# The order in which the last projection streams its 512 weight columns, changed in each of its four groups

## The reference

```python
def conv_ffn(h, w_up, conv_w, w_down):
    ...
    gate, val = jnp.split(c, 2, axis=-1)
    return (jax.nn.silu(gate) * val) @ w_down          # (256, 5632) @ (5632, 2048)
...
        x = x + rms_norm(conv_ffn(h, ffn_w_up[i], ffn_conv[i], ffn_w_down[i]), norm_g[i, 3])
```

## Time and profile before

| | us |
|---|---|
| median of 3 runs (2315.87, 2316.13, 2316.15) | 2316.13 |
| span of the profiled execution | 2315.1 |
| what lies around the span (median less span) | 1.0 |
| PE busy in the span | 2301.6 |
| DVE busy | 1535.4 |
| ACT busy | 1074.0 |
| first start of the last projection's matmuls | 2058.82 |
| start of its last matmul | 2307.46 |

### The profile page before, as it was taken

The page is one execution under the profiler, slowest core; times in us unless marked ns, Lnnn a source line. Parts: engine busy times, 40 slices in busy tenths (PEclk is TensorE's granted clock), DMA queues, the critical chain, the costliest instruction groups (busy, mean ns, idle before and its releaser), DMA issues.

```text
span 2315.1 us, 49304 instructions
## 1 busy us (share of the span) xinstructions
PE 2301.6 (99%) x19362; PEld 2100.1 (91%) x19362; DVE 1535.4 (66%) x1976; ACT 1074.0 (46%) x1365; POOL 111.5 (5%) x144
## 2 busy tenths in 40 slices
PE   9999999999999999999999999999999999999998
PEld 9999999999999999998889999899888888888887
DVE  5688877748766666665444867648877877774444
ACT  5543344455444444443444555655444444444343
POOL 2000000012000000000000200012000000000000
PEclk9999999999999999999999999999999999999999
DMA  7554334455666666666666574465655565666664
GB/s 253 172 165 123 119 103 125 132 196 173 192 184 183 187 186 184 181 191 187 187 189 184 156 246 128 121 198 155 191 190 191 180 196 176 192 189 201 190 184 153
DMA packets 115833, 406.94 MB, mean 176 GB/s; under 512 B 13008, under 2 KB 17968, under 8 KB 115312
## 3 DMA queue, kind: packets, MB, share of 16 engines
q1 hardware_dynamic: 110672, 396.03, 55.4%
q10 hardware_dynamic: 5024, 8.87, 1.1%
HBM read 402.70 MB, written 2.15 MB: 175 GB/s over the span
## 4 chain that ended last, share of the span: by engine, by line
PE 95%; DVE 2%; DMA 1%; POOL 1%; ACT 1%; issue 0%; DVEq 0%; POOLq 0%; ACTq 0%
PE ps L1895 25%; PE ps L1897 13%; PE ps L1900 8%; PE ps L1901 8%; PE ps L1902 8%; PE ps L2548 4%; PE ps L2549 4%; PE ps L2550 4%; PE ps L2094 3%; PE ps L2084 2%; PE ps L2085 2%; PE ps L2086 2%; PE ps L1859 2%; PE ps L1858 2%; PE ps L1857 2%; PE ps L2450 1%
## 5 line engine op out<-in xcount | busy, mean ns | idle before, releaser
L1047 DVE TENSOR_TENSOR wl<-raw,wh 128x1024 fp32r<-128x1024 f32 x742 | 906.1, 1233 | 653.2 <-ACT wh L581 651.7
L581 ACT ACTIVATE wh<-raw 128x1024 fp32r<-128x1024 f32 x742 | 776.0, 1057 | 885.1 <-PE ps L1897 362.1
L1895 PE MATMUL ps<-x,wh 128*128 128x512 f32 x1280 | 448.2, 393 | 0.8 <-DVE wl L1047 0.8
L1900 PE MATMUL ps<-xx,wh 128*128 128x258 f32 (+3 forms) x1336 | 379.9, 284 | 2.1 <-DVE xx L1080 1.2
L1901 PE MATMUL ps<-xx,wh 128*128 128x258 f32 (+3 forms) x1336 | 378.3, 283 | 0.0
L1902 PE MATMUL ps<-xx,wl 128*128 128x258 f32 (+3 forms) x1336 | 377.8, 283 | 0.0
L1897 PE MATMUL ps<-x,wl 128*128 128x256 f32 x1280 | 357.1, 279 | 0.0
L1895 PEld LDWEIGHTS ps<-x,wh 128*128 128x128 f32 x1280 | 239.8, 187 | 58.6 <-DVE wl L1047 1.1
L1900 PEld LDWEIGHTS ps<-xx,wh 128*128 128x128 f32 x1336 | 251.3, 188 | 4.7 <-DVE wl L1047 2.3
L1901 PEld LDWEIGHTS ps<-xx,wh 128*128 128x128 f32 x1336 | 251.3, 188 | 0.4
L1902 PEld LDWEIGHTS ps<-xx,wl 128*128 128x128 f32 x1336 | 251.4, 188 | 0.0
(11 more groups left out here) (354 smaller groups left out, 3848.8 us busy)
## 6 DMA issues: line engine op xcount, KB each, us to landing
raw<-in_gate_up SPq DMA_DIRECT2D x176, 512.0 KB, 3.6
raw<-in_down SPq DMA_DIRECT2D x176, 512.0 KB, 4.2
raw<-in_up SPq DMA_DIRECT2D x176, 512.0 KB, 3.9
raw<-in_w_in SPq DMA_DIRECT2D x103, 512.0 KB, 3.7
raw<-in_in SPq DMA_DIRECT2D x48, 512.0 KB, 3.6
raw<-in_w_out SPq DMA_DIRECT2D x32, 512.0 KB, 4.4
raw<-in_out SPq DMA_DIRECT2D x32, 512.0 KB, 3.7
bias<-bias_rows ACTq DMA_DIRECT2D x1, 4096.0 KB, 26.5
```

Source lines behind the costliest of these rows:

```text
L581: act.activation(wh[:, slot], raw[:, slot], ACT.Copy).then_inc(high_ready, 1)
L1047: dve.tensor_tensor(wl[:, slot], raw[:, slot], wh[:, slot].bitcast(F32), ALU.subtract).then_inc(low_ready, 1)
L1895: pe.matmul(ps[:, 4 * parity + m, :].rearrange("p (s n) -> p s n", s=2), w_high, hi, start=(k == 0), stop=False)
L1900: pe.matmul(out, w_high, high, start=(k == 0), stop=False)
```

## The change

Each group of `down2` gets an entry of the table `STREAM`: a number of streams, a run length, and a side. The 512 columns are cut into so many streams, and the walk takes a run from each in turn. For "read" the address pattern of the streaming operand does this: with two streams of 16 it reads columns 0 to 15, 256 to 271, 16 to 31, 272 to 287, and so on, and the sums go to PSUM as before, one after the other. The host stores the weight columns so that each lands in its place. For "write" the weights are read one after the other, and the address pattern of the output in PSUM jumps in the same manner. Group 0 reads two streams of 16, group 1 two of 8, group 2 writes two of 16, group 3 reads four of 32. No instruction is added, removed or moved, no wait and no semaphore changes, and the chunks have the same size and order. Every matmul of the four groups has 512 columns as before.

```diff
+STREAM = [(2, 16, "read"), (2, 8, "read"), (2, 16, "write"), (4, 32, "read")]
+
+def _streamed(chunks):
+    chunks = chunks.reshape(4, -1, P, 2, 512)
+    out = np.empty_like(chunks)
+    for g, (parts, run, _) in enumerate(STREAM):
+        order = np.arange(512).reshape(parts, -1, run).transpose(1, 0, 2).reshape(-1)
+        if STREAM[g][2] == "read":
+            out[g][..., order] = chunks[g]
+        else:
+            out[g] = chunks[g][..., order]
+    return np.ascontiguousarray(out.reshape(-1, P, 2, 512))
...
+            def streamed(columns, g):
+                parts, run, side = STREAM[g]
+                if side != "read":
+                    return columns
+                return columns.rearrange("p (s a b) -> p a s b", s=parts, b=run)
+
+            def written(columns, g):
+                parts, run, side = STREAM[g]
+                return columns.rearrange("p (s a b) -> p a s b", s=parts, b=run) if side == "write" else columns
...
                     out = ps[:, 2 * g + t, :]
-                    pe.matmul(out, acth[:, k, tokens], wh[:, slot, kk, :], start=(k == 0), stop=False)
-                    pe.matmul(out, acth[:, k, tokens], wl[:, slot, kk, :], start=False, stop=False)
-                    last = pe.matmul(out, actl[:, k, tokens], wh[:, slot, kk, :], start=False, stop=(k == 2 * per - 1))
+                    out = written(out, g)
+                    w_high, w_low = streamed(wh[:, slot, kk, :], g), streamed(wl[:, slot, kk, :], g)
+                    pe.matmul(out, acth[:, k, tokens], w_high, start=(k == 0), stop=False)
+                    pe.matmul(out, acth[:, k, tokens], w_low, start=False, stop=False)
+                    last = pe.matmul(out, actl[:, k, tokens], w_high, start=False, stop=(k == 2 * per - 1))
...
-        "down2": _chunks(a["ffn_w_down_2"][0]),
+        "down2": _streamed(_chunks(a["ffn_w_down_2"][0])),
```

## The result

The changed kernel took 2322.14 us in the median of 9 runs, against 2316.21 us of 9 runs before: a ratio of 1.0026, 95% interval [1.0018, 1.0034]. It is slower by 5.9 us. The forecast was no change. The time lies in the stated range, but above the 2312 to 2320 us of the forecast's own case, and the likeliest case was the wrong one.

A forecast was written before the change was run, and what follows sets the result against it. The prediction took TensorE's 1056 matmuls in the last projection to bound the kernel. The span of 2315.1 us, plus 0 for the jumps, plus 1.0 around it gave 2316.1; forecast 2316, range 2302 to 2346.

The forecast's parts named there:

- the forecast's own case: Whole kernel: the change does nothing that can be measured, 2316 us, own range 2312 to 2320; chance 0.45.
- What bounds the stage: Last projection: weights are ready before TensorE wants them, so the stage lasts as long as its 1056 matmuls, 232.4 ns each.
- Where the 19 ns go: Each matmul of the last projection: 19.1 ns above 213.3 belong to feeding, or writing, four bytes a lane in every tick.
- The price of a jump: Address jumps in the four groups' matmuls, 36,960 in all: between 0 and 1.4 ns each, taken as 0.
- the `xx` pair: Lines 1895 and 1897: matmuls of 512 columns, in two runs far apart, and 256 contiguous columns, 351.0 ns from start to start.
- The jump in PSUM: Group 2's output: no row shows a jump there, and its price was taken as the same 0.
- The rival of jumps that cost: Every jump costs a hiccup, linearly: 15.4 us at 0.42 ns each, 52 us at 1.4 ns; chance 0.26.
- The rival of relief: Streams in turn avoid the matmuls' 8% loss: half away gives 2306 us, all of it 2296; chance 0.20.

The follow-up runs named there:

- e7_all_2x1: Changed kernel with all four groups reading two streams in runs of 1: 2299.34 us against 2316.71 before, ratio 0.9925.
- e9_near: Changed kernel with walks inside few neighbouring columns (0 4 1 5…; 0 2 1 3; 0 8 1 9…) and half by half: steps 215.9, 232.4, 215.8, 215.8 ns.
- e1_writes: Changed kernel with all groups reading in one run and only the sums in PSUM jumping: 2316.51 us against 2316.66 before, ratio 1.0000.
- e6_width: Changed kernel with 96 or 64 stationary tokens: one run took 231.7 and 229.4 ns a matmul, two streams of 8 took 243.3 at both.
- e2_read_runs: Changed kernel with all groups reading two streams, in runs of 128, 64, 32 and 4: steps 232.4, 232.4, 236.7 and 249.9 ns.
- e3_read_streams: Changed kernel reading runs of 16 from four, eight and sixteen streams, fourth group in one run: steps 236.0, 241.6, 240.0 and 232.4 ns.
- e4_read_short: Changed kernel reading two streams in runs of 2 and 1, four in runs of 8 and 64: steps 326.8, 215.9, 233.4 and 232.4 ns.

## Why the prediction was wrong, point by point

**What bounds the stage** was right. The stage still lasts as long as its matmuls, the clock stays at 1.00, ACT waits for line 2577, and the change in the steps (6.05 us) is the change in the time (5.9 us).

**Where the 19 ns go** was half seen. The prediction put them on feeding or writing four bytes in each tick. e7_all_2x1 and e9_near bring the loss to 2.5 ns by the reading order alone, with the sums written and the weights loaded as before, so most of it belongs to the feeding. e1_writes adds that another order of writing changes nothing, and e6_width that half the tokens of the stationary operand take away 3.0 ns. The 16.5 and the 3.0 ns are more together than the loss of 19.1, so in part they are the same.

**The price of a jump** is the step that failed. The prediction read the `xx` pair (351.0 ns, one jump) beside `act` (351.0) and `yy` (349.6), and took 0 between 0 and 1.4 ns. (The 349.6 comes from starts rounded to 0.1 us over 47 us, so it is good to about 0.7 ns only; from starts to 0.01 us, 1487.57 and 1534.81, it is 349.9, and the bound 1.0.) The 264 x 109 = 28,776 reading jumps cost 6.05 us: 0.21 ns each in the mean. The row that was to price them could not: its jump stands after a run of 256 columns, and e2_read_runs shows that runs of 64 and more jump for nothing, while runs of 32 there, and of 16 and 8 in the change, don't. What followed from it, "the feed's mean rate seems set by how much is fed and not by where it lies", is refuted by every walk from 215.8 to 483 ns over the same 512 columns.

**The jump in PSUM** at 0 was right, for the changed group and down to runs of 2.

**The rival of jumps that cost** was right in its sign, and its bounds held the price. Its mechanism, one price for each jump, was wrong: the groups don't stand as 31 to 63 to 15 (7.7, 10.9 and 4.3 ns), the same 31 jumps cost 3.6 to 9.2 ns (e3_read_streams), and 511 jumps gain 16.5 ns (e4_read_short).

**The rival of relief** was right that an order can take away the loss, nearly to its ceiling of 20.2 us, and no walk of the change was such an order.

What stays open: why a jump behind runs of 4 to 32 costs what it does, which is the mechanism of the change's own loss; why runs of 16 from four streams (236.0) are cheaper than from two, eight or sixteen, and four of 8 (233.4) cheaper than two of 8 (243.3); and why 3 ns of the loss go with half of the stationary operand's tokens. That the order of reading costs these times is shown. The two readers are a theory that foretold four walks of e9_near to the ns; nobody has seen them, and they don't give these sizes. A walk that jumps between streams while its readers take four columns at a time was not tried.

## What to carry to other kernels

A row prices an operation only where it has the feature that costs: one jump behind 256 columns says nothing of jumps behind 16, so where no row has the feature, give the unknown its share and test it in pieces, one variant for each group of a single run. Before accepting a matmul's step as the engine's rate, compare it with columns over clock; here 8% were hidden in a stage that showed PE busy for all of its time. Where a matmul streams 512 columns of f32 data as this one does, try the order 0 4 1 5 2 6 3 7, or two halves in turn, and let whoever stores the data lay it out for that: here it took the step from 232.4 to 215.8 ns. Measure each walk, for its neighbours are dear: four single columns in turn took 280.2 ns, eight 483.4.

## What the runs showed of the hardware

The order of addresses alone moves the step of a matmul of 512 f32 columns between 215.8 and 483 ns, with the granted clock at 1.00 in the stages of both. Reading a long run in order isn't the fastest walk (232.4). The page "TensorE: Matmul & The Clock Gate" of the Trainium skill ("Back-to-back issue gap") gives N / 2.4 + 2.5 ns, an estimate of 512 / 2.4 + 2.5 = 215.8 ns here, which the kernel before missed by 16.6 and e7_all_2x1 meets. And the order in which sums land in PSUM, in runs of 16, 8 or 2, changed the step by nothing that the starts could show.
